# Prompt attention stage: two low parts on VectorE, the samples' preparation in one piece, row requests on SyncE

## What is computed

```python
u = einsum('btd,dc->btc', rms_norm(x), w_in)
u_a, u_b, u_m = split(u)
# RWKV-7 state step, per head (64 x 64 state S)
def step(S, inp):
    r_t, k_t, v_t, kk_t, a_t, w_t = inp
    sa = einsum('bhij,bhj->bhi', S, kk_t)
    S = S * w_t[:, :, None, :] - sa[..., None] * (kk_t * a_t)[:, :, None, :] \
        + v_t[..., None] * k_t[:, :, None, :]
    return S, einsum('bhij,bhj->bhi', S, r_t)
...
o = (o - mean) * rsqrt(var + GN_EPS) * gn_w + gn_b
o = o + sum(r * k * r_k) * v
o = o * silu(g)
# attention: masked softmax of q k / 8 - slope * distance, three branches, sigmoid gates
o = g[0] * o_cmp + g[1] * o_sel + g[2] * o_win
h = x + (sig(u_m_a) * (o_a @ w_pa) + sig(u_m_b) * (o_b @ w_pb)) @ w_o
```

## Time and profile before

| | us |
|---|---|
| median of 3 runs | 2412.33 |
| lowest, highest | 2409.82, 2413.7 |
| span of the profiled execution | 2410.3 |
| PE busy in it | 2253.5 |
| the stage of the change, about | 1310 to 1714 |

### The profile page before, as it was taken

How to read it: one execution, slowest core, us unless ns; L and a number is a source line. 1 busy time by engine, 2 the same in 40 slices (tenths; PEclk the granted TensorE clock), 3 DMA queues, 4 the chain that set the end, 5 groups by cost and what they waited for, 6 DMA issues and landing times. The chain is left out here.

```text
span 2410.3 us, 52252 instructions
## 1 busy us (share of the span) xinstructions
PE 2253.5 (93%) x21510; PEld 2075.3 (86%) x21510; DVE 1232.6 (51%) x2418; ACT 841.6 (35%) x1643; POOL 536.8 (22%) x401
## 2 busy tenths in 40 slices
PE   6899999999999999999999789899989769999997
PEld 4898888888888888999999678788877559999997
DVE  4244645555555554397884464444145415355454
ACT  4333333333433322222222455555223214233342
POOL 0000000000000000010100999999414410000000
PEclk8999999999999999999999899999999979999998
DMA  3321121212122122586774312211759953445564
GB/s 109 105 90 51 64 79 55 74 51 64 65 69 74 53 72 72 193 285 216 255 256 157 87 63 80 84 61 55 278 167 322 303 184 123 138 137 171 186 201 140
DMA packets 142560, 318.88 MB, mean 132 GB/s; under 512 B 27786, under 2 KB 59764, under 8 KB 141300
## 3 DMA queue, kind: packets, MB, share of 16 engines
q1 hardware_dynamic: 102148, 225.64, 28.3%
q0 software_dynamic: 16352, 54.58, 6.6%
q10 hardware_dynamic: 23824, 35.33, 4.5%
HBM read 278.26 MB, written 45.54 MB: 134 GB/s over the span
## 5 line engine op out<-in xcount | busy, mean ns | idle before, releaser
L178 PE MATMUL acc<-xh,w_hi 128*128 128x272 f32 x3008 | 671.6, 305 | 42.1 <-DVE w_lo L161 18.4
L178 PE MATMUL acc<-xh,w_lo 128*128 128x272 f32 x3008 | 628.7, 291 | 0.0
L178 PE MATMUL acc<-xl,w_hi 128*128 128x272 f32 x3008 | 628.2, 291 | 0.0
L178 PEld LDWEIGHTS acc<-xh,w_hi 128*128 128x128 f32 x3008 | 475.6, 192 | 100.3 <-issue 54.2
L178 PEld LDWEIGHTS acc<-xl,w_hi 128*128 128x128 f32 x3008 | 480.3, 192 | 0.0
L178 PEld LDWEIGHTS acc<-xh,w_lo 128*128 128x128 f32 x3008 | 477.6, 192 | 0.0
L161 DVE TENSOR_TENSOR w_lo<-w_raw,w_hi 128x1024 fp32r<-128x1024 f32 x164 | 200.5, 1224 | 217.7 <-ACT w_hi L153 215.9
L153 ACT ACTIVATE w_hi<-w_raw 128x1024 fp32r<-128x1024 f32 x188 | 198.6, 1056 | 297.6 <-PE acc L178 201.5
L2634 DVE TENSOR_TENSOR m_w_lo<-m_w,m_w_hi 128x1024 fp32r<-128x1024 f32 x96 | 117.6, 1225 | 141.4 <-ACT m_w_hi L2569 141.4
L1267 DVE SCALAR_TENSOR_TENSOR b_C<-b_rows,b_pos_s,b_C 128x512 f32<-128x512 f32 x240 | 162.5, 746 | 0.0
L2759 PE MATMUL m_acc<-m_m_hi,m_w_hi 128*128 128x272 f32 x512 | 154.0, 301 | 0.0
(11 more groups left out here) (415 smaller groups left out, 3419.5 us busy)
## 6 DMA issues: line engine op xcount, KB each, us to landing
w_raw<-in_w_all SPq DMA_DIRECT2D x168, 512.0 KB, 3.6
m_w<-in_w_mo SPq DMA_DIRECT2D x96, 512.0 KB, 3.9
b_rows<-in_cmp_rows SPq DMA_DIRECT2D x128, 256.0 KB, 3.7
w_raw<-in_w_all ACTq DMA_DIRECT2D x20, 512.0 KB, 5.5
tmp_uT<-ub ACTq DMA_DIRECT2D x35, 272.0 KB, 3.3
m_gates<-tmp_uT SPq DMA_DIRECT2D x32, 272.0 KB, 2.7
d_ring<-in_sel_k SPq DMA_DIRECT2D x64, 128.0 KB, 4.4
d_ring<-in_sel_k POOLq DMA_DIRECT2D x64, 128.0 KB, 4.4
```

The lines of the kernel that those rows point to most:

```text
L178: ins = self.nc.tensor.matmul(acc[:, c, 0:HALF], w[:, k % KH, :], x[:, k, c * HALF:(c + 1) * HALF], start=(k == 0 and m == 0), stop=(k == ...
```

## The change

Low parts 142 and 143 move from GpSimd to VectorE, where they stand ahead of the stage's `enter`. GpSimd starts its count at half 144: it waits for low part 143, makes low part 144, and then begins the steps. The samples' preparation on VectorE is done in one piece ahead of the steps (the bonus term and the gate included), and GpSimd's steps wait for all of it and for all three of ScalarE's functions, whose order is now sigmoid, square root, exponential. The row requests move from ScalarE to SyncE: rows 0 and 1 among the first loads, row `w + 2` after the raw tiles that are due by row `w`'s last tile and after VectorE has taken that tile's scores.

```diff
     def act_before(act):
...
-        f(w[:, :, :], sw, ACT.Exp, scale=DECAY_SCALE).then_inc(act_done, 1)
+        f(gate[:, :, :], g, ACT.Sigmoid).then_inc(act_done, 1)
         act.wait_ge(norm_in, 1)
         f(ss[:, :], ss[:, :], ACT.Sqrt).then_inc(act_done, 1)
-        f(gate[:, :, :], g, ACT.Sigmoid).then_inc(act_done, 1)
+        f(w[:, :, :], sw, ACT.Exp, scale=DECAY_SCALE).then_inc(act_done, 1)
...
         pool.wait_ge(ready, 1)
-        pool.wait_ge(act_done, 1)
+        pool.wait_ge(act_done, 3)
         pool.wait_ge(state_in, 16)
...
-            if t == 0:
-                pool.wait_ge(ready, 2)
...
+        link(tt(rk[:, :, :], r, k2[:, :, :], ALU.mult))
+        link(tt(rk[:, :, :], rk[:, :, :], over_t(2), ALU.mult))
         dve.wait_ge(act_done, 2)
         link(vv.reciprocal(ss[:, :], ss[:, :]))
         link(tt(kk[:, :, :], kraw[:, :, :], over_d(ss), ALU.mult))
+        link(red(bonus[:, :], rk[:, :, :]))
+        link(tt(b[:, :, :], kk[:, :, :], a, ALU.mult))
+        link(tt(rk[:, :, :], v, over_d(bonus), ALU.mult))
+        link(tt(gate[:, :, :], gate[:, :, :], g, ALU.mult))
         dve.sem_inc(ready, 1)
-        link(tt(b[:, :, :], kk[:, :, :], a, ALU.mult))
-        dve.sem_inc(ready, 1)
...
             enter(sp)
+            load_row(sp, 0)
             load_keys(0)
+            load_row(sp, 1)
             load_values(0)
             load_group(1)
...
                 background(place["S1", last])
+                if w + 2 < len(ROWS):
+                    taken(sp, ("S1", last), ("C", w))
+                    load_row(sp, w + 2)
...
-            lows, steps = [W.h0 + 2], [0]
+            lows, steps = [W.h0 + 4], [0]
...
             load_samples(pool)
+            pool.wait_ge(W.w_lo, lows[0])
             W.low(pool, lows[0])
...
             enter(act)
-            load_row(act, 0)
...
-            load_row(act, 1)
             samples_act(act)
...
-                    if (u + 1) % N_TILE == N_TILE - 1 and w + 2 < len(ROWS):
-                        load_row(act, w + 2)
...
+            for h in (W.h0 + 2, W.h0 + 3):
+                W.low(dve, h)
             enter(dve)
             v.memset(tiny[:, :], 1e-30).then_inc(tiny_set, 1)
-            samples_rest = samples_dve(dve)
+            samples_dve(dve)
...
-                if u >= 8 and samples_rest:
-                    samples_rest.pop(0)()
```

More of the change, by code:

```diff
@@ L1475, in dve_before @@
         link(tt(kk[:, :, :], kraw[:, :, :], over_d(ss), ALU.mult))
+        link(red(bonus[:, :], rk[:, :, :]))
+        link(tt(b[:, :, :], kk[:, :, :], a, ALU.mult))
+        link(tt(rk[:, :, :], v, over_d(bonus), ALU.mult))
+        link(tt(gate[:, :, :], gate[:, :, :], g, ALU.mult))
         dve.sem_inc(ready, 1)
-        link(tt(b[:, :, :], kk[:, :, :], a, ALU.mult))
-        dve.sem_inc(ready, 1)
[L1480 to L1488, removed]
+        link.restart()
     def dve_after(dve):
```

## The result

| | before | after |
|---|---|---|
| median, us | 2411.94 | 2431.76 |
| lowest, highest | 2409.82, 2413.7 | 2430.99, 2432.63 |
| executions | 4 | 4 |
| the profiled execution's own time | 2412.33 | 2432.63 |
| its span | 2410.3 | 2430.7 |

No record names the time of the profiled execution before; 2412.33 is the one that lies 2.0 us above its span, as 2432.63 lies 1.9 above the one after. The ratio is 1.0083, with a 95% interval of 1.007 to 1.0095. The change makes the kernel 19.8 us slower. 2427 was forecast, with a range of 2416.5 to 2436.

The account below looks back on a forecast made before the run. PE's and GpSimd's nearly tight chains were taken to bound prompt attention. Row 12's 15.9 us lateness, less 3.3 of saved ScalarE waits, plus 2.7 of lost clock, gave +15.3 on 2412.3: 2427 us, range 2416.5 to 2436.

Parts of the forecast that it names:

- Part 1: Stage start: low parts 142 and 143 on VectorE remove PE's 11.85 us wait and the 2.7 us of lost clock.
- What is late next: After the stage's start: ScalarE waits for raw tiles 144 and 146 before row 0's exponentials; gain some 6 us by then.
- Part 2: GpSimd's chain: low part 144 ahead of its first step makes it 8.0 us late; alone this moves the end +3.9 us.
- W: Time when raw tile 144 lands, taken as 1335.3, with bounds of 1331 and 1343.9.
- Q: GpSimd's lateness at its second big step, W - 1327.3, put at 8.0 us (3.7 to 16.6).
- Part 3: Samples' preparation moved to where GpSimd is idle: a gain of about 8 us on PE, at 1405.
- The sum: Whole span: 2410.3 + 15.3 = 2425.6 us, from the stage ending 15.3 us later; forecast 2427 us.
- Part 4: Rows on SyncE: saves about 1.1 us per row, but rows wait behind low parts; row 12 comes 15.9 us later.
- row r behind low part 144 + r, and 6.0 us to land: SyncE's queue: rows 2 to 9 wait for that low part, rows 10 to 15 for 145 + r, then land 6 us later.
- 10 us or so at row 2: Sign at the row scores: PE waits that long for row 2's DMA load, 14 at row 3, again at rows 11 and 12.
- rival A: Prompt attention: rows are in time, GpSimd alone decides; 2416.2 to 2418.9, say 2418 us; chance 0.18.
- Behind the stage everything is released by PE, and shifts as a whole: After prompt attention: the rest of the span moves by the stage end's shift, with nothing added.

Follow-up runs that it names:

- part 3 alone: The kernel before with only the samples' preparation on VectorE done in one piece ahead of GpSimd's steps; 2413.03 us, ratio 1.0002.
- part 4 alone: The kernel before with only the row requests moved from ScalarE to SyncE; 2429.44 us, ratio 1.0075.
- low part 144 on VectorE: The changed kernel, rows on SyncE, with low part 144 made by VectorE instead of GpSimd; 2418.36 us, ratio 1.0024.
- parts 1 and 3: The changed kernel with only the row requests put back on ScalarE; 2421.12 us, ratio 1.0036.
- one load earlier, low 144 after the step: The changed kernel with row requests one weight load earlier on SyncE and low part 144 made after GpSimd's first step; 2423.14 us, ratio 1.0048.
- low 144 on VectorE, rows on ScalarE: The changed kernel with row requests back on ScalarE and low part 144 made by VectorE; 2408.72 us, ratio 0.9993.
- low 144 on VectorE, one load earlier: The changed kernel with low part 144 made by VectorE and row requests one weight load earlier on SyncE; 2416.95 us, ratio 1.002.
- low 144 on VectorE, rows on ScalarE, count of 20: The changed kernel, rows back on ScalarE, low part 144 on VectorE, GpSimd's low parts spread over its steps raised from 19 to 20; 2408.97 us, ratio 0.9987.

## Why the prediction was right

**Part 1** went as said: the 11.85 us are gone, and PE is at row 0 by 1331.32. "What is late next" was ScalarE: PE waits 14.11 us for row 0's exponentials, which stand behind high parts 144 (from 1335.51) and 146 (from 1343.05), each started late for its raw tile, as said.

**Part 2.** W was taken as 1335.3, and the high part of half 144 starts at 1335.51; Q was 8.0 and is 8.2. The bounds were made for one big stall on SyncE's list or two. There were two smaller ones, 4.10 and 4.54 us; the tile was asked for at 1330.93, between the 1327.2 and 1337.4 of the two bounds, and its high part started 4.6 us later. That 1335.3 was met to 0.2 us in a range of 13 is luck: the tile was asked for 3.0 us later than before and its high part followed 2.0 us sooner on the request, and nothing in the prediction says that these two would nearly cancel. That GpSimd alone would cost 3.9 us agrees with the stage end of +3.3 when the rows are on ScalarE.

**Part 3.** The 8 us were 7.7, and worth nothing at the end (part 3 alone). The sum had put them at nothing there too, since row 12 stands behind its low part.

**Part 4** carried the sum, and its step holds: "row r behind low part 144 + r, and 6.0 us to land". It measured 5.9 and 6.1 us at rows 3 and 12 of the changed kernel, 6.2 and 5.9 with part 4 alone, 6.8 and 6.7 with low part 144 on VectorE. Row 3 was put at 1421 and came at 1420.94; row 12 at 1610.2 and came at 1610.05. The stage's end was put at +15.3 and is +15.7. What the sum has wrong is how its terms would act one by one: it adds GpSimd's 8.0 us to the order on SyncE, so part 4 alone should have given +7 at the stage's end, and gave +14.8, since a PE that is late at row 3 makes GpSimd late as well. The two hits at rows 3 and 12 don't show that the 8.0 us were needed. The waits on the way there were less well forecast: "10 us or so at row 2" were 2.4, and row 11 waited 1.6. PE had lost that time already, by a wait that I had not seen. ScalarE and PE of the changed kernel:

```profile
1371.17 1.06 ACT L153 ACTIVATE w_hi<-w_raw 128x1024 fp32r<-128x1024 f32 x1 [7.68 <-DMA w_raw<-in_w_all]
...
1372.44 0.69 PE L1885 MATMUL a_bank<-ident,a_S 128*128 128x128 f32 x2 [6.47 <-ACT a_PTc L1732]
```

It is the way through the raw tile and the high part again. It changed nothing, since row 3's gate doesn't depend on how early PE is.

The rule of the Trainium skill that the prediction set against this ("DMA: Bandwidth & Descriptors", issuing engines are not separate DMA queues) gave rival A's 2418 as long as it is read to mean that part 4 costs nothing, and that reading is not borne out here: part 4 alone cost 18 us. What it says of the shared DMA engines is neither shown nor refuted: a row's last transfer landed in 3.6 us from SyncE's queue, against 3.1. What decided was the wait ahead of the request on its own queue.

**The mis-sized term** is "Behind the stage everything is released by PE, and shifts as a whole": 0 was put, and 20.4 - 15.7 = 4.7 us came on top. Here are two stretches of work behind the stage and the whole rest of the span, in the kernel before and then in the changed one, shifted by 15.7 us. The last three numbers are the granted clock, the DMA share and GB/s:

```profile
1714.00:1760.00 46.00, 39.99 (x296) 39.55 (x295) 10.29 (x9) 12.95 (x17) 14.98 (x27) 0.93 0.88 300
1760.00:1800.00 40.00, 33.38 (x276) 28.36 (x274) 16.64 (x33) 9.23 (x17) 5.39 (x10) 0.91 0.42 133
1714.00:2410.30 696.30, 628.50 (x5388) 592.61 (x5386) 305.59 (x433) 223.76 (x332) 98.98 (x177) 0.95 0.59 196
```

```profile
1729.70:1775.70 46.00, 40.50 (x291) 40.06 (x290) 10.29 (x9) 12.69 (x17) 14.98 (x27) 0.89 0.87 299
1775.70:1815.70 40.00, 34.48 (x268) 30.46 (x270) 14.55 (x26) 8.73 (x15) 4.31 (x8) 0.87 0.39 120
1729.70:2430.70 701.00, 632.73 (x5388) 596.46 (x5386) 305.67 (x433) 223.34 (x332) 98.91 (x177) 0.94 0.59 194
```

The clock is 0.93 and 0.91 in the two stretches before, and 0.89 and 0.87 in the changed kernel, where the evacuation at 1807.69 before comes at 1825.48: the shift has grown from 15.7 to 17.8 us there. For the same 5388 matmuls behind the stage PE is busy 632.73 us where it was 628.50. So 4.2 of the 4.7 us are slower matmuls, and 0.5 us is idle time. In the profiled execution of every kernel with the count of 19 or 20 whose trace is read, the span moved by more than the stage's end did, never by less. The last column is how much longer than 628.5 us PE is busy behind the stage:

| kernel | stage end | span | between | PE busy |
|---|---|---|---|---|
| changed | +15.7 | +20.4 | 4.7 | +4.2 |
| parts 1 and 3 | +3.3 | +3.7 | 0.4 | +0.2 |
| part 4 alone | +14.8 | +17.3 | 2.5 | +0.5 |
| one load earlier, low 144 after the step | +7.4 | +8.9 | 1.5 | 0.0 |
| part 3 alone | -0.2 | +4.0 | 4.2 | +2.9 |
| low 144 on VectorE, rows on ScalarE | -4.2 | -2.9 | 1.3 | +0.8 |
| low 144 on VectorE, one load earlier | +1.8 | +7.2 | 5.4 | +3.9 |
| low 144 on VectorE | +5.5 | +8.6 | 3.1 | +1.0 |
| low 144 on VectorE, rows on ScalarE, count of 20 | -8.2 | -2.3 | 5.9 | +0.6 |

It isn't a matter of the shift alone, since part 3 by itself has 4.2 of it. In the last row it is nearly all idle time, the waits for VectorE's low parts told above. In the changed kernel it is slower matmuls at a lower granted clock; what lowers the clock stays open, and no run was made for it. Each row is one execution, and executions of one kernel differ by as much: the kernel before took 2408.67 to 2418.98 us in ten. With the rows back on ScalarE the profiled execution is the shortest of seven, 2415.98, with a mean granted clock of 0.972, and the median is 2421.12; the other six, at 0.968 to 0.971, left no trace. So the stage end of +3.3, which meets the 3.9 of the prediction's part 2, and the 2421.12, which misses the expected 2415 to 2418, are not of the same execution.

## What to carry to other kernels

In this kernel a request cost what stood ahead of it on its queue, not the 2.2 us that four of them take to issue. Before moving one to an idle engine, look at that engine's waits: an engine that "only requests" and waits 351.1 us in a stage is not free, and program order turns each of its waits into a wait of the moved request. Where two chains are tight, a gain on one is worth only the other's slack (7.7 us came to 0.2, 14.9 to 2.3), so ask first what the other chain's last member is, and how late it may be.

## What the runs showed that I had not expected

- Raising GpSimd's count by three cost 17 to 29 us, and by one it was harmless (2.7 us of waits). A background task that is put in by a count of steps blocks its engine as soon as it comes ahead of its inputs.
- A moved call can be without effect where another call has already emitted the same work: two of 14 rows kept their place, and PE waited 5.22 and 10.72 us at these two, with no wait left at the others.
- Behind the stage, where nothing is changed, the kernels differ by 0.4 to 5.9 us, with the granted clock in the same work at 0.93 in one and 0.89 in another.
